# High and low weight halves interleaved word by word in one tile, so that the stationary operand is read with a step of two words

## The chip, the cores and the metric

The program runs on one NeuronCore of one Trainium2 chip, as one launch. The metric is the device time of that launch in microseconds; lower is better. The kernel before takes 2504.3 us, the median of 3 runs (2500.88 to 2507.38).

## What is computed

The reference chains two transformer stacks of two layers each over 512 tokens of width 1024 (528 with 16 meta tokens in the first stack). All arrays are float32. Cut to the products that matter here:

```
first:  h @ w_in_ab, attention with a top-k indexer, gated linear attention, @ w_out_ab
        h @ w_in_cd, retention, stick-breaking attention, @ w_out_cd
second: x = x + 0.5 * swiglu(rms_norm(x), w_gate, w_up, w_down)     # four times, width 2816
        x = x + pool_mla_mixer(...)      # layer 0
        x = x + gated_conv_mixer(...)    # layer 1
def swiglu(x, w_gate, w_up, w_down):
    return (jax.nn.silu(x @ w_gate) * (x @ w_up)) @ w_down
```

## The kernel before, in words

Activations live transposed: features on the 128 partitions, tokens along the free dimension (tiles `NH`, `NL`, `GH`, `GL`, `MH`, `ML`). The large products are all made with float32r operands, and each is split into three: with a weight w = wh + wl and an activation x = xh + xl, where the h part is the value rounded to float32r and the l part the rest, the kernel adds wh·xh + wh·xl + wl·xh in PSUM. A matmul and the weight load before it are written with one call; the first operand behind the output is the stationary one, which is loaded into the array (the PEld rows of the profile), the second is the moving one, which streams past it (the PE rows).

All weights are cut into blocks of up to 1024 rows by 256 columns (class `Block`, in the order of `weight_plan`). `raw`, `wh` and `wl` each have two slots; block b uses slot b % 2. For each block:

- SyncE's queue loads `raw` (`load_block`), once the low parts of block b - 2 are made.
- ScalarE (ACT) writes `wh` from `raw` with a Copy (`split_high`, L622: one instruction of up to 128x2048), once TensorE has finished block b - 2.
- GpSimd (POOL) writes `wl` = `raw` - `wh` (`split_low`, L641: four instructions of 128x512, two k tiles each), and counts `weights_low`.
- TensorE waits for `weights_low` and runs the block (`gemm`, `gemm_k`).

The form of a block says which operand is stationary and how wide the moving one is. In forms "F" (L667, 512 tokens), "W" (L660, 264 tokens, twice), "H" (L664, 264 tokens) and in `gemm_halves` (L689) the weights are stationary and the activations move. In forms "T0" and "T1" (L670) the activations are stationary and 256 columns of `wh` or `wl` move. Form "S" is a gate block of the swiglu products: it is made by the seven products of Strassen's scheme (`seven_pe`, L554), 84 matmuls with 256 moving tokens instead of 96. For it POOL and VectorE (DVE) first form sums of quarters of the weights in `ssum` (L509, L510, L515, L517), then ACT and POOL split the seven left operands (`seven_high`, L530; `seven_low`, L535): four of them into quarters of `wh` and `wl`, the other three into the tiles `swh` and `swl` (three quarters each). There are 36 such blocks, nine for each of the four swiglu stages, and each is followed by an "F" block of the up projection.

A block's steps sit in one queue per engine and in the order of the blocks, so ACT's and POOL's splits of block b + 1 run while TensorE works on block b. TensorE's instructions are in one fixed order, written out by the program. In every 512 token product the k loop is outermost and the three parts follow one another:

```
        for n, (w, x) in enumerate(((wh, hi), (wh, lo), (wl, hi))):
            ...
                last = nc.tensor.matmul(ps[0:m1 - m0, bank, 0:SEQ], w[:, s, k, m0:m1], x(k), start=start, stop=stop)
```

In `wh` and `wl` the 128 words of a stationary operand lie side by side in each partition.

Of the kernel before, what the change touches and what calls it, by code (L numbers as in the profile page):

```python
# [12 lines left out]
P = 128  # L13
# [248 lines left out]
def program(nc, inp, const_in, buckets_in, out, bias_line):  # L262
# [17 lines left out]

    H = at("H", 0, [P, KT, T])
    raw = at("raw", 4224, [P, 2, KT, BC])
    wh = at("wh", 8320, [P, 2, KT, BC], F32R)
    wl = at("wl", 12416, [P, 2, KT, BC], F32R)
    XA, XB = 16512, 20736
    K = [at("K0", 24960, [P, CONST_DATA[0].shape[1]]), None, None, None]
    gain = at("gain", 25600, [P, NROWS + 8])
# [137 lines left out]
    thi = at("thi", 34432, [P, 4, QT, QN], F32R)  # L425
    tsum = at("tsum", 30336, [P, 4, QT, QN])
    tlo = at("tlo", 30336, [P, 4, QT, QN], F32R)
    swh = at("swh", 38528, [P, 3, QT, P], F32R)
    swl = at("swl", 40064, [P, 3, QT, P], F32R)
    ssum = at("ssum", 41600, [P, 4, QT, P])  # L430
    xs = at("xs", 43648, [P, 3, QN])
    gcb = at("gcb", 29744, [P, 2, SEQ])
# [50 lines left out]
    def blk_cols(b):  # L483
        blk = BLOCKS[b]
        c0, n, to = blk.cols[-1]
        return to + n

    def seven_raw(b, name):
        row, col = int(name[1]) - 1, int(name[2]) - 1
        return raw[:, b % 2, QT * col:QT * col + QT, P * row:P * row + P]  # L490

    def seven_full(b, name):
        return seven_raw(b, name) if name[0] == "A" else ssum[:, int(name[1]) - 1, :, :]

    def seven_left(b, name, tile, extra):
        if name[0] == "A":
            row, col = int(name[1]) - 1, int(name[2]) - 1
            return tile[:, b % 2, QT * col:QT * col + QT, P * row:P * row + P]
        return tile[:, b % 2, 0:QT, P:2 * P] if name == "S1" else extra[:, int(name[1]) - 2, :, :]

    def seven_right(name, plain, formed):
        if name[0] == "B":
# [16 lines left out]
    def seven_high(act, b):  # L519
        n = SEVENS.index(b)  # L520
        act.wait_ge(S(f"raw_ready_{b % 2}"), RAWC[b])
        act.wait_ge(S("unit_done"), units_before(b - 1))
        for name in LEFT:
            if name == "S1":
                act.wait_ge(S("gate_sum"), 2 * n + 2)
            elif name == "S2":
                act.wait_ge(S("gate_mix"), 2 * n + 1)
            elif name == "S4":
                act.wait_ge(S("gate_mix"), 2 * n + 2)
            nc.scalar.activation(seven_left(b, name, wh, swh), seven_full(b, name), ACT.Copy).then_inc(S("weights_high"), 1)  # L530

    def seven_low(pool, b):
        for j, name in enumerate(LEFT):
            pool.wait_ge(S("weights_high"), HIGH_BEFORE[b] + j + 1)
            nc.gpsimd.tensor_tensor(seven_left(b, name, wl, swl), seven_full(b, name), seven_left(b, name, wh, swh).bitcast(F32),  # L535
                                    ALU.subtract).then_inc(S("weights_low"), 1)

    def seven_pe(pe, b, f, first):

        u, n = BLOCKS[b].unit0, SEVENS.index(b)  # L540
        for j, (left, right) in enumerate(zip(LEFT, RIGHT)):
            pe.wait_ge(S("weights_low"), LOW_BEFORE[b] + j + 1)
            if left == "A11":
                wait_slot(pe, u)
            elif left in ("S2", "S4", "S3"):
                pe.wait_ge(S("gate_copy"), 3 * n + ("S2", "S4", "S3").index(left) + 1)
            elif left == "A22":
                pe.wait_ge(S("gate_mid"), n + 1)
            if first and right[0] == "T":
                pe.wait_ge(S("formed_low"), 4 * f + T_ORDER.index(right) + 1)  # L550
            o = ps[:, ACCUMULATOR[j], 0:QN]
            for k in range(QT):
                for x, (w, e, plain, formed) in enumerate(((wh, swh, NH2, thi), (wh, swh, NL2, tlo), (wl, swl, NH2, thi))):
                    last = nc.tensor.matmul(o, seven_left(b, left, w, e)[:, k, :], seven_right(right, plain, formed)[:, k, :],  # L554
                                            start=left in ("A11", "S1", "A12") and k == 0 and x == 0,
                                            stop=k == QT - 1 and x == 2, skip_group_check=True)
# [54 lines left out]
    def split_high(act, b):  # L611

        if b >= len(BLOCKS):
            return
        if BLOCKS[b].form == "S":
            seven_high(act, b)
            return
        act.wait_ge(S(f"raw_ready_{b % 2}"), RAWC[b])
        if b >= 2:
            act.wait_ge(S("unit_done"), units_before(b - 1))  # L620
        k, w = BLOCKS[b].kts, blk_cols(b)
        nc.scalar.activation(wh[:, b % 2, 0:k, 0:w], raw[:, b % 2, 0:k, 0:w], ACT.Copy).then_inc(S("weights_high"), 1)  # L622

    def split_first_high(act, h):
        ks = slice(4 * h, 4 * h + 4)
        act.wait_ge(S("raw_ready_0" if h else "raw_first"), 16)
        nc.scalar.activation(wh[:, 0, ks, :], raw[:, 0, ks, :], ACT.Copy).then_inc(S("weights_high" if h else "first_high"), 1)

    def split_low(pool, b):
        if BLOCKS[b].form == "S":  # L630
            seven_sums_pool(pool, b)
            seven_low(pool, b)
            return
        if b:
            pool.wait_ge(S("weights_high"), HIGH_BEFORE[b + 1])
        k, w = BLOCKS[b].kts, blk_cols(b)
        for k0 in range(0, k, 2):
            if b == 0 and k0 % 4 == 0:
                pool.wait_ge(S("weights_high" if k0 else "first_high"), 1)
# [9 lines left out]
    def gemm_k(pe, b, i, k, hi, lo):  # L649

        blk = BLOCKS[b]
        s, total = b % 2, blk_cols(b)
        bank = bank_of(blk.unit0 + i)
        for n, (w, x) in enumerate(((wh, hi), (wh, lo), (wl, hi))):
            start, stop = k == 0 and n == 0, k == blk.kts - 1 and n == 2
            if blk.form == "W":
                m0, m1 = i * P, min(total, i * P + P)
                for h in range(2):
                    last = nc.tensor.matmul(ps[0:m1 - m0, bank + h, 0:T // 2], w[:, s, k, m0:m1],  # L660
                                            x(k)[:, h * (T // 2):(h + 1) * (T // 2)], start=start, stop=stop)
            elif blk.form == "H":
                m0, c0 = i // 2 * P, i % 2 * (T // 2)
                last = nc.tensor.matmul(ps[:, bank, 0:T // 2], w[:, s, k, m0:m0 + P], x(k)[:, c0:c0 + T // 2], start=start, stop=stop)  # L664
            elif blk.form == "F":
                m0, m1 = i * P, min(total, i * P + P)
                last = nc.tensor.matmul(ps[0:m1 - m0, bank, 0:SEQ], w[:, s, k, m0:m1], x(k), start=start, stop=stop)  # L667
            else:
                c0, n_tok = token_tile(i) if blk.form == "T1" else (i * P, P)
                last = nc.tensor.matmul(ps[0:n_tok, bank, 0:total], x(k)[:, c0:c0 + n_tok], w[:, s, k, 0:total], start=start, stop=stop)  # L670
        if k == blk.kts - 1:
            last.then_inc(S("unit_done"), 1)

    def gemm_halves(pe, b, hi, lo, ready):

        blk = BLOCKS[b]
        pe.wait_ge(S("weights_low"), LOW_BEFORE[b + 1])
        for i in range(2):
            wait_slot(pe, blk.unit0 + i)
        wide = blk.form == "W"  # L680
        w = T // 2 if wide else SEQ // 2
        for h in range(2):
            ready(pe, h)
            for i in range(2):
                bank = bank_of(blk.unit0 + i)
                o = ps[:, bank + h, 0:w] if wide else ps[:, bank, h * w:(h + 1) * w]
                for k in range(blk.kts):
                    for n, (weights, x) in enumerate(((wh, hi), (wh, lo), (wl, hi))):
                        last = nc.tensor.matmul(o, weights[:, b % 2, k, i * P:(i + 1) * P], x(k)[:, h * w:(h + 1) * w],  # L689
                                                start=k == 0 and n == 0, stop=k == blk.kts - 1 and n == 2)  # L690
                if h:
                    last.then_inc(S("unit_done"), 1)
# [2187 lines left out]
```

## Time and profile before

| | |
|---|---|
| runs | 2507.38, 2504.3, 2500.88 us |
| profiled execution | span 2503.9 us from its first to its last instruction; no other time is given for it |
| TensorE matmul (PE) | busy 2457.6 us, 98%, 14279 instructions |
| TensorE weight load (PEld) | busy 2087.2 us, 83%, 14279 instructions |
| GpSimd (POOL) | busy 1374.0 us, 55% |
| VectorE (DVE) | busy 1211.0 us, 48% |
| ScalarE (ACT) | busy 1007.4 us, 40% |
| mean granted TensorE clock | 0.995 of full speed |

Busy time of PE is from modelled ends: two matmuls in sequence overlap in the records, so a matmul's own duration says little, and the distance from one start to the next is what it costs the engine. The chain of waits, printed in order of time, merges the uninterrupted matmuls of one line into one row with their count; its microseconds divided by the count give that distance.

### The profile page before, as it was taken

The numbers are of one execution on the slowest core, as the hardware profiler recorded it, in microseconds if no ns is written. First come the engines' busy times: TensorE is split into PE (matmuls) and PEld (weight loads), VectorE is DVE, ScalarE is ACT, GpSimd is POOL, SyncE is SP. The second block draws the span as 40 slices with busy tenths as digits, with TensorE's granted clock in tenths as the row PEclk, the third lists the DMA queues.
The fourth block names the chain that finished last, engine by engine and source line by source line (L and its number), as shares of the span: only waits on it lengthen the run. The fifth ranks groups of instructions, "written<-read, shape, count | busy, mean of one in ns | idle before, by whom it ended". The sixth has DMA issues, their size and how long they took to land.

```text
span 2503.9 us, 35008 instructions
## 1 busy us (share of the span) xinstructions
PE 2457.6 (98%) x14279; PEld 2087.2 (83%) x14279; DVE 1211.0 (48%) x1948; ACT 1007.4 (40%) x1658; POOL 1374.0 (55%) x1010
## 2 busy tenths in 40 slices
PE   8999999999999999999999999999999999999999
PEld 7899779876678888877688988888988888888887
DVE  5666444245576242456573434462524543633333
ACT  4423444246563333437553433442423312433331
POOL 4233344421258686643167767586766454568673
PEclk9999999999999999999999999999999999999999
DMA  4223103210133333322123232323332322232322
GB/s 139 67 68 94 35 24 121 81 55 18 44 103 102 101 102 101 95 63 74 35 90 115 93 107 85 117 84 106 96 102 89 114 95 91 84 118 85 118 84 85
DMA packets 215881, 217.90 MB, mean 87 GB/s; under 512 B 10615, under 2 KB 213106, under 8 KB 215722
## 3 DMA queue, kind: packets, MB, share of 16 engines
q1 hardware_dynamic: 215520, 215.61, 27.1%
q8 instruction: 114, 1.87, 0.3%
q14 instruction: 45, 0.37, 0.0%
q10 hardware_dynamic: 202, 0.06, 0.0%
HBM read 213.53 MB, written 2.12 MB: 86 GB/s over the span
## 4 chain that ended last, share of the span: by engine, by line
PE 89%; DVE 5%; ACT 3%; POOL 1%; issue 1%; DMA 1%; SPq 0%; DVEq 0%; ACTq 0%
PE ps L667 53%; PE ps L554 14%; PE ps L660 6%; PE ps L670 5%; PE ps L664 2%; PE ps L1020 2%; ACT wh L622 1%; PE ps L1055 1%; POOL wl L641 1%; DVE tsum L599 1%; PE ps L1037 1%; PE ps L2317 1%; PE ps L2378 1%; PE ps L1818 1%; ACT bf L588 0%
## 5 line engine op out<-in xcount | busy, mean ns | idle before, releaser
L641 POOL TENSOR_TENSOR wl<-raw,wh 128x512 fp32r<-128x512 f32 (+1 forms) x650 | 863.9, 1359 | 1046.4 <-ACT wh L622 1031.7
L667 PE MATMUL ps<-NH,wh 128*128 128x512 f32 (+1 forms) x1248 | 493.3, 395 | 5.0 <-POOL wl L641 2.8
L667 PE MATMUL ps<-NL,wh 128*128 128x512 f32 (+1 forms) x1248 | 488.5, 391 | 0.0
L667 PE MATMUL ps<-NH,wl 128*128 128x512 f32 (+1 forms) x1248 | 487.6, 391 | 0.0
L622 ACT ACTIVATE wh<-raw 128x2048 fp32r<-128x2048 f32 (+5 forms) x182 | 310.6, 1707 | 430.5 <-PE ps L667 330.8
L667 PE MATMUL ps<-GH,wh 128*128 128x512 f32 x824 | 323.0, 392 | 0.0
L667 PE MATMUL ps<-GH,wl 128*128 128x512 f32 x824 | 320.7, 389 | 0.0
L667 PE MATMUL ps<-GL,wh 128*128 128x512 f32 x824 | 320.7, 389 | 0.0
L667 PEld LDWEIGHTS ps<-NH,wh 128*128 128x128 f32 (+1 forms) x1248 | 234.8, 188 | 61.0 <-issue 8.0
L667 PEld LDWEIGHTS ps<-NH,wl 128*128 128x128 f32 (+1 forms) x1248 | 234.7, 188 | 50.9
L667 PEld LDWEIGHTS ps<-NL,wh 128*128 128x128 f32 (+1 forms) x1248 | 234.8, 188 | 49.2 <-issue 1.4
L1292 DVE SCALAR_TENSOR_TENSOR H<-ps,H 128x512 f32<-128x512 f32 x96 | 66.4, 691 | 310.9 <-PE ps L667 310.8
L535 POOL TENSOR_TENSOR wl<-raw,wh 128x512 fp32r<-128x512 f32 x108 | 173.6, 1621 | 27.6 <-ACT wh L530 27.6
L667 PEld LDWEIGHTS ps<-GH,wh 128*128 128x128 f32 x824 | 154.7, 188 | 32.8 <-issue 1.0
L667 PEld LDWEIGHTS ps<-GH,wl 128*128 128x128 f32 x824 | 154.7, 188 | 32.3
L667 PEld LDWEIGHTS ps<-GL,wh 128*128 128x128 f32 x824 | 154.7, 188 | 31.4
L535 POOL TENSOR_TENSOR swl<-ssum,swh 128x512 fp32r<-128x512 f32 x108 | 154.2, 1459 | 0.0
L530 ACT ACTIVATE wh<-raw 128x512 fp32r<-128x512 f32 x108 | 63.7, 621 | 178.2 <-PE ps L667 72.0
L1284 DVE TENSOR_TENSOR GL<-tmp,GH 128x512 fp32r<-128x512 f32 x88 | 74.4, 845 | 102.2 <-ACT GH L1242 102.2
L1242 ACT ACTIVATE GH<-tmp 128x512 fp32r<-128x512 f32 x88 | 55.4, 629 | 158.8 <-DVE tmp L1282 158.7
L1282 DVE TENSOR_TENSOR tmp<-sg,tmp 128x512 f32<-128x512 f32 x88 | 88.7, 1008 | 36.3 <-ACT sg L1235 33.8
L670 PE MATMUL ps<-wh,NH 128*128 128x256 f32 (+1 forms) x320 | 90.9, 284 | 0.2 <-ACT dv L1995 0.2
(470 smaller groups left out, 5038.9 us busy)
## 6 DMA issues: line engine op xcount, KB each, us to landing
raw<-in_ffn_w_gate SPq DMA_DIRECT2D x44, 1024.0 KB, 5.3
raw<-in_ffn_w_up SPq DMA_DIRECT2D x44, 1024.0 KB, 5.3
raw<-in_ffn_w_down SPq DMA_DIRECT2D x32, 1024.0 KB, 5.1
raw<-in_w_in_ab SPq DMA_DIRECT2D x15, 1024.0 KB, 5.4
raw<-in_w_in_cd SPq DMA_DIRECT2D x14, 1024.0 KB, 5.0
raw<-in_ffn_w_down SPq DMA_DIRECT2D x16, 768.0 KB, 4.4
raw<-in_c_w_in SPq DMA_DIRECT2D x12, 1024.0 KB, 5.1
raw<-in_w_out_ab SPq DMA_DIRECT2D x8, 512.0 KB, 3.4
```

The source lines that it names most:

```text
L530: nc.scalar.activation(seven_left(b, name, wh, swh), seven_full(b, name), ACT.Copy).then_inc(S("weights_high"), 1)
L535: nc.gpsimd.tensor_tensor(seven_left(b, name, wl, swl), seven_full(b, name), seven_left(b, name, wh, swh).bitcast(F32), ALU.subtract).then ...
L554: last = nc.tensor.matmul(o, seven_left(b, left, w, e)[:, k, :], seven_right(right, plain, formed)[:, k, :], start=left in ("A11", "S1", " ...
L622: nc.scalar.activation(wh[:, b % 2, 0:k, 0:w], raw[:, b % 2, 0:k, 0:w], ACT.Copy).then_inc(S("weights_high"), 1)
L641: nc.gpsimd.tensor_tensor(wl[:, b % 2, ks, 0:w], raw[:, b % 2, ks, 0:w], wh[:, b % 2, ks, 0:w].bitcast(F32), ALU.subtract).then_inc(S("wei ...
L660: last = nc.tensor.matmul(ps[0:m1 - m0, bank + h, 0:T // 2], w[:, s, k, m0:m1], x(k)[:, h * (T // 2):(h + 1) * (T // 2)], start=start, sto ...
L667: last = nc.tensor.matmul(ps[0:m1 - m0, bank, 0:SEQ], w[:, s, k, m0:m1], x(k), start=start, stop=stop)
L670: last = nc.tensor.matmul(ps[0:n_tok, bank, 0:total], x(k)[:, c0:c0 + n_tok], w[:, s, k, 0:total], start=start, stop=stop)
L1242: nc.scalar.activation(GH[:, 2 * p_ + i, :], tmp[:, i, 0:SEQ], ACT.Copy).then_inc(S("hidden_high"), 1)
L1282: nc.vector.tensor_tensor(tmp[:, i, 0:SEQ], sg[:, i, :], tmp[:, i, 0:SEQ], ALU.mult).then_inc(S("hidden"), 1)
L1284: nc.vector.tensor_tensor(GL[:, 2 * p_ + i, :], tmp[:, i, 0:SEQ], GH[:, 2 * p_ + i, :].bitcast(F32), ALU.subtract).then_inc(S("hidden_low" ...
L1292: nc.vector.scalar_tensor_tensor(out=H[:, m, META:T], in0=ps[:, bank_of(u), :], scalar=0.5, in1=H[:, m, META:T], op0=ALU.mult, op1=ALU.add ...
```

## The change

The two tiles `wh` and `wl` become one piece of memory of the same size at the same place. For each slot it is seen in two ways: `w_pairs`, in which word 2c is the high half and word 2c + 1 the low half of column c, and `w_rows`, in which all high words of a slot lie in front of all its low words. `weights_of(b, low)` takes `w_rows` for the forms T0 and T1, where the weights are the moving operand, and `w_pairs` for every other form. `swh` and `swl` become `sw_pairs` in the same way. So in the forms F, W, H and S each stationary operand is 128 words at a step of two words; ACT's Copy writes at that step; POOL's subtraction reads the high halves and writes the low ones at that step, and reads `raw` or `ssum` as before. The number of instructions on each engine, their order, their element counts and their waits stay as they were.

```diff
-    wh = at("wh", 8320, [P, 2, KT, BC], F32R)
-    wl = at("wl", 12416, [P, 2, KT, BC], F32R)
+    w_pairs = at("w_pairs", 8320, [P, 2, KT, BC, 2], F32R)
+    w_rows = at("w_rows", 8320, [P, 2, 2, KT, BC], F32R)
...
-    swh = at("swh", 38528, [P, 3, QT, P], F32R)
-    swl = at("swl", 40064, [P, 3, QT, P], F32R)
+    sw_pairs = at("sw_pairs", 38528, [P, 3, QT, P, 2], F32R)
...
+    def weights_of(b, low):
+        return w_rows[:, b % 2, low, :, :] if BLOCKS[b].form[0] == "T" else w_pairs[:, b % 2, :, :, low]
+
...
-    def seven_left(b, name, tile, extra):
+    def seven_left(b, name, low):
+        tile = weights_of(b, low)
         if name[0] == "A":
             row, col = int(name[1]) - 1, int(name[2]) - 1
-            return tile[:, b % 2, QT * col:QT * col + QT, P * row:P * row + P]
-        return tile[:, b % 2, 0:QT, P:2 * P] if name == "S1" else extra[:, int(name[1]) - 2, :, :]
+            return tile[:, QT * col:QT * col + QT, P * row:P * row + P]
+        return tile[:, 0:QT, P:2 * P] if name == "S1" else sw_pairs[:, int(name[1]) - 2, :, :, low]
...
-        nc.scalar.activation(wh[:, b % 2, 0:k, 0:w], raw[:, b % 2, 0:k, 0:w], ACT.Copy).then_inc(S("weights_high"), 1)
+        nc.scalar.activation(weights_of(b, 0)[:, 0:k, 0:w], raw[:, b % 2, 0:k, 0:w], ACT.Copy).then_inc(S("weights_high"), 1)
...
-            nc.gpsimd.tensor_tensor(wl[:, b % 2, ks, 0:w], raw[:, b % 2, ks, 0:w], wh[:, b % 2, ks, 0:w].bitcast(F32), ALU.subtract).then_inc(S("weights_low"), 1)
+            nc.gpsimd.tensor_tensor(weights_of(b, 1)[:, ks, 0:w], raw[:, b % 2, ks, 0:w], weights_of(b, 0)[:, ks, 0:w].bitcast(F32), ALU.subtract).then_inc(S("weights_low"), 1)
...
-        for n, (w, x) in enumerate(((wh, hi), (wh, lo), (wl, hi))):
+        for n, (low, x) in enumerate(((0, hi), (0, lo), (1, hi))):
+            w = weights_of(b, low)
...
-                last = nc.tensor.matmul(ps[0:m1 - m0, bank, 0:SEQ], w[:, s, k, m0:m1], x(k), start=start, stop=stop)
+                last = nc.tensor.matmul(ps[0:m1 - m0, bank, 0:SEQ], w[:, k, m0:m1], x(k), start=start, stop=stop)
```

## Rows read from the trace of the kernel before

**Rows 1.** The page: span, busy time per engine, granted TensorE clock
```profile
span 2503.9 us, 35008 instructions
...
PE 2457.6 (98%) x14279; PEld 2087.2 (83%) x14279; DVE 1211.0 (48%) x1948; ACT 1007.4 (40%) x1658; POOL 1374.0 (55%) x1010
...
PEclk9999999999999999999999999999999999999999
```

**Rows 2.** The page: the chain that ended last, by engine and line
```profile
PE 89%; DVE 5%; ACT 3%; POOL 1%; issue 1%; DMA 1%; SPq 0%; DVEq 0%; ACTq 0%
PE ps L667 53%; PE ps L554 14%; PE ps L660 6%; PE ps L670 5%; PE ps L664 2%; PE ps L1020 2%; ACT wh L622 1%; PE ps L1055 1%; POOL wl L641 1%; DVE tsum L599 1%; PE ps L1037 1%; PE ps L2317 1%; PE ps L2378 1%; PE ps L1818 1%; ACT bf L588 0%
```

**Rows 3.** TensorE's waits: engine, line, waited for, us, times, longest
```profile
PE ps L667 <- POOL wl L641: 2.8, 6, 1.0
```

**Rows 4.** Chain in order of time: start us, us, what
```profile
458.70 19.48 PE ps L667 x84
478.19 23.48 PE ps L660 x192
...
1303.92 10.07 PE ps L554 x84
1313.99 10.91 PE ps L667 x48
...
1334.97 54.43 PE ps L667 x240
...
1170.05 1.75 PE ps L1657 x16
```

**Rows 5.** Groups, PE by shape (line, names, sizes, count | busy us, mean ns)
```profile
L667 PE MATMUL ps<-NH,wh 128*128 128x512 f32 x1240 | 490.1, 395 | 5.0 <-POOL wl L641 2.8 <-DVE NL L777 2.2
...
L667 PE MATMUL ps<-GH,wh 128*128 128x512 f32 x824 | 323.0, 392 | 0.0
...
L554 PE MATMUL ps<-thi,swh 128*128 128x256 f32 x288 | 81.6, 283 | 3.5 <-ACT xs L566 2.0 <-issue 1.5
...
L660 PE MATMUL ps<-NH,wh 128*128 128x264 f32 x304 | 64.9, 295 | 2.7 <-DVE agT L1979 2.7
...
L554 PE MATMUL ps<-NH,swh 128*128 128x256 f32 x144 | 40.8, 283 | 0.0
...
L664 PE MATMUL ps<-NH,wh 128*128 128x264 f32 x128 | 38.9, 304 | 0.0
...
L660 PE MATMUL ps<-MH,wh 128*128 128x264 f32 x112 | 25.8, 312 | 0.1
```

**Rows 6.** Groups, weight loads (PEld) by shape
```profile
L667 PEld LDWEIGHTS ps<-GL,wh 128*128 128x128 f32 x824 | 154.7, 188 | 31.4
...
L670 PEld LDWEIGHTS ps<-wh,NH 128*16 128x16 f32 x64 | 6.0, 94 | 2.1 <-issue 0.8
```

**Rows 7.** Timeline of POOL over one S and F pair, 1510 to 1531 us
```profile
1510.10 3.79 POOL L535 TENSOR_TENSOR swl<-ssum,swh 128x512 fp32r<-128x512 f32 x3
1513.86 2.53 POOL L535 TENSOR_TENSOR wl<-raw,wh 128x512 fp32r<-128x512 f32 x2
1518.93 5.05 POOL L641 TENSOR_TENSOR wl<-raw,wh 128x512 fp32r<-128x512 f32 x4 [2.54 <-ACT wh L622]
1523.94 1.29 POOL L509 TENSOR_TENSOR ssum<-raw 128x512 f32<-128x512 f32 x1
1525.19 1.29 POOL L510 TENSOR_TENSOR ssum<-raw 128x512 f32<-128x512 f32 x1
1527.72 1.74 POOL L535 TENSOR_TENSOR wl<-raw,wh 128x512 fp32r<-128x512 f32 x1 [1.24 <-ACT wh L530]
1529.42 1.74 POOL L535 TENSOR_TENSOR wl<-ssum,wh 128x512 fp32r<-128x512 f32 x1
```

**Rows 8.** Timeline of ACT, the same pair
```profile
1516.94 1.91 ACT L622 ACTIVATE wh<-raw 128x2048 fp32r<-128x2048 f32 x1 [5.72 <-PE ps L667]
...
1527.01 0.63 ACT L530 ACTIVATE wh<-raw 128x512 fp32r<-128x512 f32 x1 [5.44 <-PE ps L554]
```

More of the change, by code:

```diff
@@ L529, in seven_high @@
                 act.wait_ge(S("gate_mix"), 2 * n + 2)
-            nc.scalar.activation(seven_left(b, name, wh, swh), seven_full(b, name), ACT.Copy).then_inc(S("weights_high"), 1)
+            nc.scalar.activation(seven_left(b, name, 0), seven_full(b, name), ACT.Copy).then_inc(S("weights_high"), 1)
     def seven_low(pool, b):
@@ L534, in seven_low @@
             pool.wait_ge(S("weights_high"), HIGH_BEFORE[b] + j + 1)
-            nc.gpsimd.tensor_tensor(seven_left(b, name, wl, swl), seven_full(b, name), seven_left(b, name, wh, swh).bitcast(F32),
+            nc.gpsimd.tensor_tensor(seven_left(b, name, 1), seven_full(b, name), seven_left(b, name, 0).bitcast(F32),
                                     ALU.subtract).then_inc(S("weights_low"), 1)
@@ L552, in seven_pe @@
             for k in range(QT):
-                for x, (w, e, plain, formed) in enumerate(((wh, swh, NH2, thi), (wh, swh, NL2, tlo), (wl, swl, NH2, thi))):
-                    last = nc.tensor.matmul(o, seven_left(b, left, w, e)[:, k, :], seven_right(right, plain, formed)[:, k, :],
+                for x, (low, plain, formed) in enumerate(((0, NH2, thi), (0, NL2, tlo), (1, NH2, thi))):
+                    last = nc.tensor.matmul(o, seven_left(b, left, low)[:, k, :], seven_right(right, plain, formed)[:, k, :],
                                             start=left in ("A11", "S1", "A12") and k == 0 and x == 0,
@@ L626, in split_first_high @@
         act.wait_ge(S("raw_ready_0" if h else "raw_first"), 16)
-        nc.scalar.activation(wh[:, 0, ks, :], raw[:, 0, ks, :], ACT.Copy).then_inc(S("weights_high" if h else "first_high"), 1)
+        nc.scalar.activation(weights_of(0, 0)[:, ks, :], raw[:, 0, ks, :], ACT.Copy).then_inc(S("weights_high" if h else "first_high"), 1)
     def split_low(pool, b):
@@ L652, in gemm_k @@
         blk = BLOCKS[b]
-        s, total = b % 2, blk_cols(b)
+        total = blk_cols(b)
         bank = bank_of(blk.unit0 + i)
-        for n, (w, x) in enumerate(((wh, hi), (wh, lo), (wl, hi))):
+        for n, (low, x) in enumerate(((0, hi), (0, lo), (1, hi))):
+            w = weights_of(b, low)
             start, stop = k == 0 and n == 0, k == blk.kts - 1 and n == 2
@@ L659, in gemm_k @@
                 for h in range(2):
-                    last = nc.tensor.matmul(ps[0:m1 - m0, bank + h, 0:T // 2], w[:, s, k, m0:m1],
+                    last = nc.tensor.matmul(ps[0:m1 - m0, bank + h, 0:T // 2], w[:, k, m0:m1],
                                             x(k)[:, h * (T // 2):(h + 1) * (T // 2)], start=start, stop=stop)
@@ L663, in gemm_k @@
                 m0, c0 = i // 2 * P, i % 2 * (T // 2)
-                last = nc.tensor.matmul(ps[:, bank, 0:T // 2], w[:, s, k, m0:m0 + P], x(k)[:, c0:c0 + T // 2], start=start, stop=stop)
+                last = nc.tensor.matmul(ps[:, bank, 0:T // 2], w[:, k, m0:m0 + P], x(k)[:, c0:c0 + T // 2], start=start, stop=stop)
             elif blk.form == "F":
                 m0, m1 = i * P, min(total, i * P + P)
-                last = nc.tensor.matmul(ps[0:m1 - m0, bank, 0:SEQ], w[:, s, k, m0:m1], x(k), start=start, stop=stop)
+                last = nc.tensor.matmul(ps[0:m1 - m0, bank, 0:SEQ], w[:, k, m0:m1], x(k), start=start, stop=stop)
             else:
                 c0, n_tok = token_tile(i) if blk.form == "T1" else (i * P, P)
-                last = nc.tensor.matmul(ps[0:n_tok, bank, 0:total], x(k)[:, c0:c0 + n_tok], w[:, s, k, 0:total], start=start, stop=stop)
+                last = nc.tensor.matmul(ps[0:n_tok, bank, 0:total], x(k)[:, c0:c0 + n_tok], w[:, k, 0:total], start=start, stop=stop)
         if k == blk.kts - 1:
@@ L687, in gemm_halves @@
                 for k in range(blk.kts):
-                    for n, (weights, x) in enumerate(((wh, hi), (wh, lo), (wl, hi))):
-                        last = nc.tensor.matmul(o, weights[:, b % 2, k, i * P:(i + 1) * P], x(k)[:, h * w:(h + 1) * w],
+                    for n, (low, x) in enumerate(((0, hi), (0, lo), (1, hi))):
+                        last = nc.tensor.matmul(o, weights_of(b, low)[:, k, i * P:(i + 1) * P], x(k)[:, h * w:(h + 1) * w],
                                                 start=k == 0 and n == 0, stop=k == blk.kts - 1 and n == 2)
```

## The prediction

> **What bounds the kernel now.** I read the page first, then the chain of waits, then the distance from matmul to matmul. On the page TensorE is busy 98% of the span and its clock is granted in full in every slice [rows 1], so neither another engine nor the clock holds the kernel back. The chain that ended last lies on PE for 89%, and three quarters of the span are the four lines whose stationary operand the change touches: L667, L554, L660 and L664 [rows 2]. TensorE hardly waits for the engine that finishes the weights: 2.8 us in all at L667 [rows 3]. So the time moves only if one matmul becomes dearer or cheaper, or if the splits get so slow that TensorE starts to wait for them.
>
> What does one matmul cost? Dividing the pieces of the chain by their counts: 54.43 / 240 = 226.8 ns for 512 moving columns, 10.07 / 84 = 119.9 ns for 256, 23.48 / 192 = 122.3 ns for 264 [rows 4]. At the granted 2.4 GHz one column per cycle gives 213.3, 106.7 and 110.0 ns. So each of these matmuls costs 12.3 to 13.5 ns more than its columns, whatever its width. Two rows say what kind of cost this is. 
>
> **The mechanism I forecast.** A weight load of 128 columns lasts 188 ns, one of 16 columns 94 ns [rows 6]: (188 - 94) / 112 = 0.84 ns per column, half the pace of the moving stream (0.42 ns per column). Both read four bytes per column from the same partitions. At a step of one word the moving read thus runs through addresses twice as fast as the stationary read and passes it again and again; if the two collide where they meet in the same part of the memory, that is a loss that depends on addresses, as seen. At a step of two words the stationary read covers eight bytes per 0.84 ns, exactly the moving read's speed: they keep their distance and collide once per load at most. The slow transposes, where the streams have another ratio of speeds, show about what is left.
>
> The Trainium skill speaks against this (TensorE: Matmul & The Clock Gate, Step-by-step: what each phase is for): TensorE has two independent read ports, and loading the next weights takes no read bandwidth from the running matmul. By that rule the gain is 0 and the time 2504 us; it is the first rival. The 5 ns that hang on the address alone do not agree with it.
>
> **The change part by part.**
> - Stationary reads at two words. Matmuls concerned: L667 3 x (1240 + 824) = 6192, L554 9 x 288 + 3 x 144 = 3024, L660 3 x (304 + 112) = 1248, L664 3 x 128 = 384 [rows 5]; 10848 in all. Each group's partners with the other two parts have the same count; some 360 in small groups are left out. The price is not in the trace, so from both sides: gain at most 13.4 - 2.7 = 10.7 ns each (116 us), at least 0; a loss is not excluded either, and is priced under the rivals. I take 9 ns, near the upper end, because the nearest row is the transposes' and I leave 1.7 ns for the one collision at a load's start: 10848 x 9 ns = 98 us. All of it lies on the path, since these lines are the chain.
> - L670 (weights moving) stays at a step of one word on both sides: nothing.
> - ACT's writes at two words. The F split takes 1.91 us for 2048 columns, the seven S splits 0.63 us each [rows 8]. Lower bound: no change. Upper bound, doubled: the F split ends 1.9 us later, the first S split 0.6 us later. Both push POOL, which idles 2.54 us before the one and 1.24 us before the other [rows 7]. I take nothing; the cover is POOL's idle time.
> - POOL's reads and writes at two words. In one pair of an S and an F block (10.07 + 10.91 = 21.0 us of TensorE [rows 4]) POOL spends 3.79 + 2.53 + 5.05 + 1.74 + 1.74 = 14.9 us on splits and 2.6 us on sums, and idles 3.8 us [rows 7]. After the forecast gain the pair is 132 x 9 ns = 1.2 us shorter and the idle time 2.6 us: still enough. The same POOL instruction on 128x512 takes 1.27 us in some rows and 1.74 us in others [rows 7], so its bounds are 0 and, if all pay the dear price, (1.74 - 1.27) x 11 = 5.2 us at most, of which part is paid already. I take nothing. What would be late next is the first low part of the S block.
> - DVE, the DMA queues, the waits and the order are as before: nothing.
>
> Sum: 2503.9 - 98 = 2406 us. The median of the runs, 2504.3, is 0.4 us above the span, which changes nothing. Own range of this case: 2385 us (10.7 ns, with the small groups) to 2465 us (a third of the loss goes).
>
> **Rivals.**
> 1. *No change, 2504 us.* The 13 ns are a fixed price of a float32r matmul whose weights are exchanged. For it: L554 with 256 columns and L667 with 512 lose the same, although the streams meet for different times; against it: 231.9 beside 226.8 ns. A measurement here can tell some 0.3% (8 us) from nothing. ACT and POOL as above stay hidden. The Trainium skill (SBUF — State Buffer, A bandwidth-pool intuition that's wrong, the box on cachelines) says that fp32 may be strided for free while two accesses fall in one 16-byte line, which a step of two words just keeps; no row here has such a step.
> 2. *More collisions, about 2600 us.* A step of two words touches twice the stretch of memory per load. If each stretch costs the moving read something, the loss grows: by 5.1 ns as between 226.8 and 231.9 (+55 us, 2559) or by another 13.4 ns (+145 us, 2649). Against it: a load of few columns does not make its neighbours free.
> 3. *The splits become the bound, about 2630 us.* Place: POOL in the S and F pairs. It decides from 3.8 / 14.9 = 26% on. At 50% dearer the splits add 7.4 us, 3.6 us of it uncovered, in 36 pairs: +130 us. TensorE would stand before L554 or L667 waiting for the low parts. Against it: one word per element is moved either way.
> 4. *The weight load becomes the bound, about 3000 us.* If a column at two words takes 1.68 instead of 0.84 ns, 128 take 215 ns and with the 13 ns no matmul can follow in less than 228. The 512-column ones stay (226.8), but 4656 of 256 or 264 columns pay 107 ns more: +498 us. It decides once 128 columns take over 120 ns, 12% more than now.
>
> **How the numbers follow.** Forecast case 50%, no change 24%, more collisions 9%, POOL 10%, weight load 7%. The likeliest case gives 2406 us. The range runs from 2375, a little below the full removal, over the forecast case and the unchanged time to 2560, the mild end of rival 2; above it lie the dear ends, rivals 3 and 4, some 20%. Faster by over 0.3%: 0.50; within: 0.24; slower: 0.26.
>
> **What would show it.** In the chain in order of time, 240 matmuls of L667's successor should take about 52.3 us instead of 54.43, 84 of L554's about 9.3 instead of 10.07, and the stretch of the first stack's F blocks (231.9 ns) should fall most. L670's distance stays. POOL's and ACT's mean durations should stay within 25% and TensorE's waits for the low parts within a few us. Wrong if the distances stay at 226.8 and 119.9 (rival 1), rise (rivals 2 and 4; in rival 4 the 256-column ones alone, with loads far over 188 ns), or if waits for POOL appear (rival 3).

## The result, and the profile after

The change makes the kernel slower: 2552.72 us, the median of 4 runs (2550.02 to 2556.5), against 2505.16 us of the kernel before beside it (2500.88 to 2507.38). The ratio is 1.0196, with a 95% interval of 1.0182 to 1.021. I had forecast 2406 us. The time moved the other way. The range holds it only at its far end, beside the mild end of rival 2 (2559 us).

The page of the kernel after, in the same parts as [rows 1]:

```profile
span 2551.6 us, 35008 instructions
...
PE 2505.3 (98%) x14279; PEld 2138.9 (84%) x14279; DVE 1210.4 (47%) x1948; ACT 1041.2 (41%) x1658; POOL 1393.7 (55%) x1010
...
PEclk9999999999999999999999999999999999999999
```

TensorE has 47.7 us more of busy time, and the span is 47.7 us longer (2551.6 - 2503.9). The clock is granted as before. Its chain and its wait for the low parts, to compare with [rows 2, 3]; L671, L557, L664 and L674 are the old L667, L554, L660 and L670:

```profile
PE 92%; DVE 4%; ACT 2%; issue 1%; POOL 1%; DMA 1%; SPq 0%; DVEq 0%; ACTq 0%
...
PE ps L671 <- POOL w_pairs L644: 1.8, 3, 0.8
```

PE's share of the chain grew from 89 to 92%, and the wait for POOL's low parts shrank from 2.8 to 1.8 us. So nobody is waited for more; TensorE's own work is dearer. Which matmuls are dearer is read from the chain in order of time (start, us, what), as [rows 4]:

```profile
458.83 19.51 PE ps L671 x84
478.34 23.58 PE ps L664 x192
...
1319.70 10.08 PE ps L557 x84
1329.77 11.31 PE ps L671 x48
...
1351.16 56.53 PE ps L671 x240
...
2006.13 179.19 PE ps L671 x768
```

- 512 columns in the swiglu stages: 56.53 / 240 = 235.5 ns, before 226.8: +8.8 ns.
- 512 columns elsewhere in the second stack: 179.19 / 768 = 233.3 ns. The same piece of the kernel before reads:

```profile
1972.57 174.11 PE ps L667 x768
```

  174.11 / 768 = 226.7 ns, so here it is +6.6 ns.
- 512 columns in the first stack, where the moving tile starts at word 16: 19.51 / 84 = 232.3 ns, before 231.9.
- 256 columns: 120.0 ns, before 119.9. 264 columns: 122.8 ns, before 122.3.

This adds up. Each of four swiglu stages has 960 such matmuls from its first S block on (nine up blocks of 48; eight down blocks of 48 and four of 36): 3840 x 8.8 = 34 us. Some 1950 others of 512 columns in the second stack: x 6.6 = 13 us. That is 47 of the 47.7 us. The starts of the same matmuls in the two traces, compared one by one, give 45.6 us for the 512 columns, 1.2 for 264 and 0.2 for 256.

The engines that write the halves, by groups. The first two rows are the kernel after, where the blocks of the forms T0 and T1 stand in a group of their own (`w_rows`), so its counts are lower:

```profile
L644 POOL TENSOR_TENSOR w_pairs<-raw,w_pairs 128x512 fp32r<-128x512 f32 x600 | 817.1, 1394 | 933.6 <-ACT w_pairs L625 920.2 <-ACT w_pairs L630 13.4
...
L625 ACT ACTIVATE w_pairs<-raw 128x2048 fp32r<-128x2048 f32 x125 | 260.8, 2086 | 335.2 <-PE ps L671 284.7 <-DMA raw<-in_ffn_w_down 25.4 <-PE ps L664 18.8
```

```profile
L641 POOL TENSOR_TENSOR wl<-raw,wh 128x512 fp32r<-128x512 f32 x639 | 854.4, 1367 | 1034.5 <-ACT wh L622 1019.8 <-ACT wh L627 13.4 <-DVE mx L1103 1.2
...
L622 ACT ACTIVATE wh<-raw 128x2048 fp32r<-128x2048 f32 x133 | 253.9, 1909 | 358.5 <-PE ps L667 277.7 <-PE ps L660 39.2 <-DMA raw<-in_ffn_w_down 29.3
```

ACT pays 9% for writing at two words (2086 against 1909 ns), POOL 2% (1394 against 1367 ns). A weight load went from 188 [rows 6] to 196 ns:

```profile
L671 PEld LDWEIGHTS ps<-GL,w_pairs 128*128 128x128 f32 x824 | 161.3, 196 | 30.3
```

### The profile page after: what moved, and what is told of

Its sections match the earlier page's. It is cut to its first block, busy times and chain, and to the rows that moved or that the text cites. A ratio compares the mean times of both kernels' runs of the same rounds, so it can differ in the third digit from the quotient of the medians.

```text
span 2551.6 us, 35008 instructions
## 1 busy us (share of the span) xinstructions
PE 2505.3 (98%) x14279; PEld 2138.9 (84%) x14279; DVE 1210.4 (47%) x1948; ACT 1041.2 (41%) x1658; POOL 1393.7 (55%) x1010
## 4 chain that ended last, share of the span: by engine, by line
PE 92%; DVE 4%; ACT 2%; issue 1%; POOL 1%; DMA 1%; SPq 0%; DVEq 0%; ACTq 0%
PE ps L671 57%; PE ps L557 14%; PE ps L664 6%; PE ps L674 4%; PE ps L668 2%; PE ps L1024 2%; PE ps L1059 1%; PE ps L1041 1%; PE ps L2321 1%; PE ps L2382 1%; PE ps L1822 1%; ACT w_pairs L625 0%; PE ps L693 0%; DVE tlo L612 0%; PE ps L2167 0%
## 5 line engine op out<-in xcount | busy, mean ns | idle before, releaser
L644 POOL TENSOR_TENSOR w_pairs<-raw,w_pairs 128x512 fp32r<-128x512 f32 (+1 forms) x608 | 824.1, 1388 | 945.1 <-ACT w_pairs L625 931.6
L671 PE MATMUL ps<-NH,w_pairs 128*128 128x512 f32 (+1 forms) x2496 | 805.2, 399 | 3.6 <-POOL w_pairs L644 1.8
L671 PEld LDWEIGHTS ps<-NH,w_pairs 128*128 128x128 f32 (+1 forms) x2496 | 487.0, 195 | 109.9 <-issue 7.8
L671 PE MATMUL ps<-GH,w_pairs 128*128 128x512 f32 x1648 | 529.8, 400 | 0.0
L671 PE MATMUL ps<-NL,w_pairs 128*128 128x512 f32 (+1 forms) x1248 | 493.9, 396 | 0.0
L625 ACT ACTIVATE w_pairs<-raw 128x2048 fp32r<-128x2048 f32 (+2 forms) x167 | 316.8, 1898 | 389.2 <-PE ps L671 321.4
L671 PEld LDWEIGHTS ps<-GH,w_pairs 128*128 128x128 f32 x1648 | 323.8, 196 | 66.2 <-issue 1.0
L671 PE MATMUL ps<-GL,w_pairs 128*128 128x512 f32 x824 | 326.2, 396 | 0.0
L671 PEld LDWEIGHTS ps<-NL,w_pairs 128*128 128x128 f32 (+1 forms) x1248 | 243.1, 195 | 47.5 <-issue 1.4
L538 POOL TENSOR_TENSOR w_pairs<-raw,w_pairs 128x512 fp32r<-128x512 f32 x108 | 177.3, 1655 | 27.4 <-ACT w_pairs L533 27.4
L671 PEld LDWEIGHTS ps<-GL,w_pairs 128*128 128x128 f32 x824 | 161.3, 196 | 30.3
L557 PE MATMUL ps<-thi,sw_pairs 128*128 128x256 f32 x576 | 115.5, 283 | 3.5 <-ACT xs L569 2.0
L674 PE MATMUL ps<-w_rows,NH 128*128 128x256 f32 (+1 forms) x640 | 117.1, 282 | 0.2 <-ACT dv L1999 0.2
L557 PE MATMUL ps<-thi,w_pairs 128*128 128x256 f32 x576 | 115.5, 283 | 0.0
L557 PE MATMUL ps<-NH,w_pairs 128*128 128x256 f32 x576 | 115.4, 283 | 0.0
L664 PE MATMUL ps<-NH,w_pairs 128*128 128x264 f32 (+1 forms) x640 | 112.5, 292 | 2.7 <-DVE agT L1983 2.7
```

Source lines behind the costliest of these rows:

```text
L538: nc.gpsimd.tensor_tensor(seven_left(b, name, 1), seven_full(b, name), seven_left(b, name, 0).bitcast(F32), ALU.subtract).then_inc(S("weig ...
L557: last = nc.tensor.matmul(o, seven_left(b, left, low)[:, k, :], seven_right(right, plain, formed)[:, k, :], start=left in ("A11", "S1", "A ...
L625: nc.scalar.activation(weights_of(b, 0)[:, 0:k, 0:w], raw[:, b % 2, 0:k, 0:w], ACT.Copy).then_inc(S("weights_high"), 1)
L644: nc.gpsimd.tensor_tensor(weights_of(b, 1)[:, ks, 0:w], raw[:, b % 2, ks, 0:w], weights_of(b, 0)[:, ks, 0:w].bitcast(F32), ALU.subtract).t ...
L671: last = nc.tensor.matmul(ps[0:m1 - m0, bank, 0:SEQ], w[:, k, m0:m1], x(k), start=start, stop=stop)
```

## The experiments

The theory after the result (A): a stationary read at two words still disturbs the moving read, more than one at one word does when both tiles start where they do here; the loss lies in TensorE's two reads alone. The rivals: (B) ACT's and POOL's writes at two words disturb TensorE's reads; (C) the weight load lasts so long that it sets the pace; (D) the new places of the halves in memory do it.

### e1_streams: the two reads with no other engine

A kernel that leaves out the reference's computation and holds series of 48 matmuls alone, in the operand pattern of the kernel (hi, lo, hi against high, high, low). ACT and POOL stand still while a series runs; only the step, the width or a start varies.

```
for step, low, n, cols, start in configs:
    for i, k, (base, x_) in ...:            # 2 x 8 x 3
        a = step * (k * 256 + i * 128) % 4096 + base
        matmul(ps[0:cols, c % 2, 0:n], w[:, a:a + cols * step:step], x_[:, k * 512 + start:k * 512 + start + n])
```

> Leaves out the whole computation; it only runs 48-matmul series, with a pause between them, on float32r operands that lie where the kernel's do (stationary words at w, moving ones at hi and lo, all at the same start modulo 2048 bytes), with the same order hi, lo, hi. Series in order: one at step 1 to warm up; then widths 512, 384, 264, 256, 128, each at stationary steps 1, 2, 4; then width 512 with the moving tiles shifted by 4, 8, 16, 32, 48, 64 words, each at steps 1 and 2; then 64 and 32 stationary columns at steps 1 and 2; then step 2 with the low half 4096, 8, 0 words away, step 1 with the low half at 0 and 4096 words, and step 2 with it at 1 word. Theory A (the two reads of TensorE meet more often at a step of two): without any other engine at work step 2 gives 233 to 236 ns per matmul at width 512 against 226.8 at step 1, and 120 for both at width 256; step 4 more than step 2. Theory B (the interleaved writes of ACT and POOL disturb TensorE): step 1 and step 2 are equal here, 226.8 ns. Fixed price theory: all shifts of the moving tile give the same distance; theory A expects it to change with the shift, by about 5 ns as between 226.8 and 231.9.

The chain in order of time of this kernel; L84 is a step of one word, L86 of two, L88 of four. The three rows of a width stand together, for 512, 256 and 128 columns:

```profile
37.92 11.19 PE ps L84 x48
...
49.41 11.48 PE ps L86 x48
...
61.18 11.69 PE ps L88 x48
...
127.55 6.02 PE ps L84 x48
...
133.88 6.05 PE ps L86 x48
...
140.22 11.49 PE ps L88 x48
...
152.01 5.59 PE ps L84 x48
...
157.90 5.88 PE ps L86 x48
...
164.08 11.48 PE ps L88 x48
```

A piece also holds a longer first step and the tail of its last matmul (0.54 us together at 512 columns), so distances are taken between starts, without the first ones. At 512 columns they are 226.7 ns at one word and 233.3 at two: the +6.6 ns of the kernel after, without ACT, POOL or a DMA at work. At 256 columns 120 and 120, at 384 columns 173.3 and 173.3, at 264 columns 121.3 and 123.2, at 128 columns 111.7 and 117.9. With the moving tile shifted by 4 to 48 words the step of one word itself costs 228.8 to 233.4 ns; shifted by 64 words it is back at 226.7. And with 64 stationary columns the step of two is the cheaper one, 226.7 against 229.8 ns. The distance between high and low half (4096, 8, 1 or 0 words) changes nothing. At four words every width costs 233 to 235 ns, as if something other than the moving columns set the pace. The load is longer there:

```profile
L88 PEld LDWEIGHTS ps<-hi,w 128*128 128x128 f32 x160 | 45.1, 325 | 2.9 <-ACT junk L68 2.9
```

It lasts 325 ns instead of 194 at two words and 193 at one. So a pace set by the load fits the series at four words, and not those at two, where 256 columns still cost 120 ns. That it is the load at four words is inferred from its length.

### e2_reads: before, with the read at two words alone

The halves stay apart and contiguous; F, W, H and `gemm_halves` load 128 words at a step of two from them, so these products use the columns of a block in another order than the reference.

```diff
+    def stepped(w, s, k, m0, m1, total):
+        return w[:, s, k, m0 // P:2 * P:2] if total == 2 * P else w[:, s, k, m0:m1]
```

> The kernel before with its layout and its writes; only in forms F, W and H the stationary operand is read at a step of two words inside the old rows: the first tile of 128 takes the even columns, the second the odd ones, so columns of the products come out permuted. Theory A: all or nearly all of the loss is there, 2545 to 2555 us, 233 to 236 ns per matmul at L667. Theory B and the placement theory: 2504 us and 226.8 ns.

Measured: 2539.12 us, ratio 1.0143 (1.0128 to 1.0158). The F blocks cost 233.2 ns without any interleaved write (L670 is the old L667):

```profile
1343.36 55.98 PE ps L670 x240
```

### e3_writes: after, with the read at one word

ACT and POOL write at two words as in the kernel after, but F, W, H and `gemm_halves` load 128 neighbouring words, which are high and low halves mixed, so these products are taken with the mixed columns. S blocks stay at two words.

```diff
+    def plain(w, b, k, low, m0, m1, total):
...
+        at_ = m0 + 2 * P * low
+        return w_pairs[:, b % 2, k, :, :].rearrange("p c t -> p (c t)")[:, at_:at_ + P]
```

> The changed kernel with its interleaved writes; only in forms F, W and H TensorE reads 128 neighbouring words of the interleaved rows, high and low mixed, so the products are of mixed halves. Theory A: about 2504 us and 226.8 ns per matmul with 512 columns. Theory B: 2545 to 2555 us. Placement theory: the same.

Measured: 2508.91 us, ratio 1.0018 (1.0007 to 1.003). ACT is as dear as in the kernel after, and TensorE is at its old distance (54.43 / 240 = 226.8):

```profile
L625 ACT ACTIVATE w_pairs<-raw 128x2048 fp32r<-128x2048 f32 x125 | 259.9, 2079 | 319.7 <-PE ps L677 271.0 <-DMA raw<-in_ffn_w_down 28.2 <-PE ps L670 18.7
```

```profile
1336.81 54.43 PE ps L677 x240
```

This refutes B but for 0.2% (4 to 5 us). Writes beside reads that are both at two words are compared further down (e6_s_rows).

### e4_place: after, with all halves in rows

```diff
-        return w_rows[:, b % 2, low, :, :] if BLOCKS[b].form[0] == "T" else w_pairs[:, b % 2, :, :, low]
+        return w_rows[:, b % 2, low, :, :]
```

> The changed kernel with the row view for every form: nothing is interleaved, but the halves lie where the change puts them (both halves of one slot side by side). Theories A and B: 2504 us. Placement theory (it is the new start addresses): 2545 to 2555 us.

Measured: 2503.89 us, ratio 1.0002 (0.9988 to 1.0016). The new places alone cost nothing; D is refuted.

### e5_grid: starts, mixtures, two-byte operands

Like e1_streams, without the reference's computation and with series of 24: 64 combinations of the starts of stationary, hi and lo (0, 16, 32, 48 words) at either step; a narrow series (84 of 256 columns, L98) and a wide one (96 of 512, L104) without a pause; bf16 operands (L112); a moving operand at one and two words (L119).

> Leaves out the whole computation; series of matmuls alone. Two series to warm up, then 64 series of 24 float32r matmuls of 512 columns at a stationary step of 1 and 64 at a step of 2, each with another start of the stationary words, of the high and of the low moving words (0, 16, 32 or 48 words past a multiple of 64, high moving tile outside, low inside, stationary outermost); then other stationary starts (4, 8, 12, 24, 40, 56 words); then steps 3, 1, 2; then four mixed series without a pause, 84 matmuls of 256 columns followed by 96 of 512, with the steps 1 1, 1 2, 2 1, 2 2; then bfloat16 operands at stationary steps 1 and 2 and widths 512 and 256; then float32r with the moving operand at steps 1 and 2, 256 columns. Theory A (collisions that depend on the distance of the two reads): over the 64 starts the distance varies from about 226.7 to 234 ns at step 1 and no start brings step 2 under 226.7; in the mixed series the wide part costs 235.5 ns after a narrow part at step 2 and 233.3 after one at step 1. Theory F (a fixed price per float32r matmul, to which a step of two adds a fixed one): the starts change nothing. The lockstep theory of the forecast: some starts at step 2 give 216 to 220 ns. For bfloat16, theory A has no firm number: 216 ns if the loss belongs to four-byte words, 227 if to every weight load.

At one word the 64 combinations give 226.7 ns (the three starts equal, and only then) to 234.5; at two words 228.8 to 233.3, in no case less. Mostly the starts relative to each other count: of 32 groups of four series with the same differences of starts, some 26 agree within 1 ns, and in the others the four differ by up to 3.5 ns. The stationary start alone is enough: 16 words later, with both moving tiles at 0, a step of one costs 233.4 ns instead of 226.7, and a step of two 230.0 instead of 233.3. The high moving tile 48 words later does the same. The first two rows are a step of one, with all starts at 0 and with the high moving one at 48 (226.7 and 234.6 ns); the other two are the same starts at a step of two (233.3 and 228.9 ns):

```profile
41.24 5.75 PE ps L89 x24
...
114.71 5.89 PE ps L89 x24
...
433.50 5.88 PE ps L89 x24
...
507.31 5.80 PE ps L89 x24
```

The mean over the 64 combinations is 231.0 ns at one word and 231.3 at two, by the starts of the matmuls in this trace. Leaving out differences of up to 0.3 ns, two words are cheaper at some 27 of the 64 and dearer at some 26. So over these starts the step itself costs next to nothing in the mean; the kernel before, with all its starts equal in the second stack, stood at one of the four combinations that favour a step of one most.

The narrow and wide series, in the order of steps (1, 1), (1, 2), (2, 1), (2, 2):

```profile
919.26 10.34 PE ps L98 x84
929.60 21.80 PE ps L104 x96
...
962.03 22.40 PE ps L104 x96
...
995.08 21.80 PE ps L104 x96
...
1027.53 22.62 PE ps L104 x96
```

The wide matmuls cost 226.7, 233.3, 226.7 and 235.6 ns. So 233.3 or 235.6 depends on what ran before: a narrow series at two words makes the wide one at two words dearer by 2.3 ns for its whole length of 96 matmuls. These are the two prices of the kernel after. In bf16 a matmul costs 216 ns with 512 columns and 109 with 256 at either step (24 take 2.81 us with 256 columns at two words), about 2.5 ns over its bare columns instead of 13. So at the one set of starts that was run in bf16, the larger loss belongs to operands of four bytes; other starts were not run in bf16.

```profile
1056.12 2.81 PE ps L112 x24
...
1064.90 2.81 PE ps L112 x24
...
1068.01 3.15 PE ps L119 x24
...
1071.46 5.71 PE ps L119 x24
```

The last two rows are 256 float32r columns moving at one and at two words: 120 and 226.6 ns. Had the change not kept `w_rows` for T0 and T1, whose weights move, those matmuls could be expected to pay this; no run tried it in the kernel.

### e6_s_rows and e7_s_only: S blocks apart from the rest

e6_s_rows is the kernel after with S blocks in rows; e7_s_only is the kernel after with S blocks alone interleaved and all else in rows.

```diff
-        return w_rows[...] if BLOCKS[b].form[0] == "T" else w_pairs[...]
+        return w_rows[...] if BLOCKS[b].form[0] in "TS" else w_pairs[...]   # e6_s_rows
+        return w_rows[...] if BLOCKS[b].form != "S" else w_pairs[...]       # e7_s_only
```

> The changed kernel, but with the gate blocks of form S in the row view (not interleaved); forms F, W and H stay interleaved. If the 235.5 ns per matmul in the swiglu stages come from S blocks read at a step of two just before (another state in which the wide series starts), L671 takes 233.3 ns everywhere and the time is 2540 to 2545 us. If they come from the interleaved writes beside the interleaved reads of the F blocks themselves, it stays at 235.5 ns and 2550 to 2553 us.

> The changed kernel, but only the gate blocks of form S are interleaved; all other forms use the row view. Theory A: matmuls with 256 columns cost 120 ns at either step, so 2503 to 2510 us, the latter if the entry state makes the wide matmuls that follow dearer. Rival 4 of the forecast (the weight load becomes the bound) expects them far over 120 ns and 2800 us or more.

e6_s_rows: 2543.95 us, ratio 1.0156 (1.0142 to 1.017). The F blocks fall to 55.98 / 240 = 233.2 ns:

```profile
1351.81 55.98 PE ps L671 x240
```

e7_s_only: 2503.32 us, ratio 1.0002 (0.9993 to 1.0011). 256-column matmuls stay at 120 ns, and the F blocks behind them, at one word, at 226.8:

```profile
1322.40 10.10 PE ps L557 x84
1332.50 54.43 PE ps L671 x240
```

So the S blocks cost nothing themselves, and rival 4 of the prediction is refuted; but at two words they make the F blocks at two words that follow them dearer. The trace of the kernel after shows the same in two more places: before its first S block its F blocks stand 233.3 ns apart, and at the end of a swiglu stage, after 216 matmuls at 50.87 / 216 = 235.5 ns, two matmuls of L816 are enough to bring the 768 that follow at 2006 us back to 233.3:

```profile
1954.26 50.87 PE ps L671 x216
2005.13 1.00 PE ps L816 x2
```

### e8_pairs_moved and e9_rows_moved: the same two moves in either kernel

`NH2` starts 48 words later and `GH` 16 words earlier, in the kernel after (e8) and in the kernel before (e9).

```diff
-    NH2 = at("NH2", XA, [P, KT, SEQ], F32R)
+    NH2 = at("NH2", XA + 48, [P, KT, SEQ], F32R)
...
-    GH = at("GH", GA + 40, [P, KT, SEQ], F32R)
+    GH = at("GH", GA + 24, [P, KT, SEQ], F32R)
```

> The changed kernel; only the high moving tiles of the second stack start elsewhere, NH2 48 words later and GH 16 words earlier, so both lie 48 words past a multiple of 64 while the low moving tiles and the weights stay at one. In the series at a step of two this start had the least loss, 228.8 ns. If the loss hangs on the starts of the two reads, L671 falls from 235.5 and 233.3 to about 229 ns in the second stack: some 5700 matmuls x 4.5 to 6.5 ns, 2518 to 2527 us. If the step costs a fixed amount, it stays at 2552 us.

> The kernel before, nothing interleaved, with the same two tiles moved in the same way. In the series at a step of one this start cost 234.4 ns against 226.7. If the loss hangs on the starts, L667 rises to about 234 ns in the second stack and the time to 2540 to 2550 us without any step of two; if a step of one is free of it, 2504 us.

e8: 2523.3 us, ratio 1.0077 (1.0062 to 1.0092), less than half of the change's loss. e9: 2538.77 us, ratio 1.0139 (1.0122 to 1.0156), with no step of two words anywhere. The F blocks of each:

```profile
1344.45 54.95 PE ps L671 x240
```

```profile
1342.33 56.26 PE ps L667 x240
```

229.0 ns at two words, 234.4 at one: at these starts the order of the two steps is turned round, as in the same four rows of e5_grid. What the change lost is in the main no price of the step as such, but of how the two reads meet at these starts.

### e10_starts, e11_all_moved, e12_formed_moved: a better start?

e10_starts: again only series, of 24 at one word, 256 combinations of the starts of hi and lo in steps of 4 words, with 512 and with 256 columns.

> Leaves out the whole computation; 512 series of 24 float32r matmuls at a stationary step of one, 256 with 512 columns and then 256 with 256 columns, the stationary words at a multiple of 64 and the high (outer loop) and low (inner loop) moving words 0, 4, 8 ... 60 words past one. It looks for a start that beats both kernels. If all starts of both reads together on a multiple of 64 words are the best there is, no series of 512 columns lies under 226.7 ns; a start near 220 ns would be worth some 40 us in the kernel. At 256 columns the kernel has 120.0; the trial with moved tiles had 118.7, so some starts should be at or under that.

512 columns: 226.6 to 236.6 ns, mean 231.8. 256 columns: 113.4 to 120.2, mean 118. With both starts at 0, where the kernel before has all its tiles of the second stack (multiples of 64 words), 512 columns cost 226.8 ns, within 0.2 ns of the least there is, and 256 columns 119.4 to 120, near the most. With both at word 28, 512 columns cost 226.7 and 256 columns 113.4:

```profile
772.53 5.72 PE ps L83 x24
```

```profile
2020.82 3.02 PE ps L83 x24
```

e11_all_moved takes this to the kernel before: right operands of the second stack 28 words later, the formed left ones 64 words later. e12_formed_moved moves only the formed operands of the S blocks.

```diff
-    thi = at("thi", 34432, [P, 4, QT, QN], F32R)
+    thi = at("thi", 34460, [P, 4, QT, QN], F32R)
...
-    tlo = at("tlo", 30336, [P, 4, QT, QN], F32R)
+    tlo = at("tlo", 30364, [P, 4, QT, QN], F32R)
...
-    NH2 = at("NH2", XA, [P, KT, SEQ], F32R)      # e11_all_moved alone,
+    NH2 = at("NH2", XA + 28, [P, KT, SEQ], F32R) # and NL2, GH, GL likewise
```

> The kernel before, nothing interleaved; all moving tiles of the second stack (NH2, NL2, GH, GL, thi, tlo, and what is formed in their place) start 28 words later, while the weights stay at multiples of 64 words (swh, swl, ssum and xs 64 words later). In the series alone this start had 226.6 ns at 512 columns and 113.4 ns at 256 (against 226.7 and 120.0 with all on a multiple of 64). If that holds beside the other engines and across the change from 256 to 512 columns: 36 blocks of 84 matmuls x 6.6 ns = 20 us less, 2484 us. If the state in which a series starts matters more than the series itself, L554 takes between 113.4 and 120 and L667 between 226.7 and 234 ns, 2490 to 2530 us.

> The kernel before, nothing interleaved; only the formed operands of the S blocks (thi, tlo and what is formed in their place) start 28 words later, NH2, NL2, GH and GL stay at multiples of 64 words. The last trial had 113.3 ns at L554's 256 columns but 231.1 at L667's 512. If the start alone counts, 48 of the 84 matmuls of an S block take 113.3 ns and 36 take 120, and L667 stays at 226.7: 36 x 48 x 6.6 ns = 11 us less, 2492 us. If the state carried over from the S block counts, L667 leaves 226.7 and the gain is gone: 2500 to 2530 us.

e11: 2507.96 us, ratio 1.0012 (1.0002 to 1.0022). The S blocks gained as hoped (9.52 / 84 = 113.3 ns), but the F blocks lost it again (55.47 / 240 = 231.1 ns, where the series at this start had 226.7):

```profile
1332.61 55.47 PE ps L671 x240
1388.07 9.52 PE ps L558 x84
...
1969.96 177.49 PE ps L671 x768
```

The S blocks are not the reason. The 768 matmuls of the last row follow two matmuls of L816 and cost 177.49 / 768 = 231.1 ns as well, and the F blocks before the first S block of the kernel stand 231.2 ns apart. What makes 231.1 of 226.7 here stays open; the series had 24 matmuls, one tile of 128 weight columns per k tile and no other engine at work, and no run separates these.

e12: 2499.56 us against 2505.04 beside it, ratio 0.9983 (0.9974 to 0.9992): a little faster than both kernels, with 54.43 and 9.92 us in the same rows. The F blocks keep their 226.8 ns beside the moved S blocks. An S matmul costs 9.92 / 84 = 118.1 ns in the mean, where the expectation gives (48 x 113.3 + 36 x 120) / 84 = 116.2, so the gain is 4 to 5 us instead of 11.

```profile
1329.29 54.43 PE ps L671 x240
1383.72 9.92 PE ps L558 x84
```

## Why the prediction was wrong, step by step

**What bounds the kernel: right.** The time moved only through the price of a matmul; waits for POOL did not appear.

**"The loss depends on where in memory the two operands lie": right.** e9_rows_moved loses 1.4% by two start addresses alone, and e1_streams shows the loss with every other engine at rest. The Trainium skill says that TensorE has two independent read ports and that loading the next weights takes no read bandwidth from the running matmul (TensorE: Matmul & The Clock Gate, Step-by-step: what each phase is for). These runs do not agree for float32r: the same instruction costs 226.6 to 236.6 ns by addresses alone, and 226.7 or 233.4 by the stationary start alone (e5_grid).

**"Stationary reads at two words", 10848 x 9 ns = 98 us gained: the step that failed.** Instead of 9 ns gained, a matmul measured 0 ns at 256 columns, +0.5 at 264, +0.4 at 512 in the first stack, and +6.6 or +8.8 at 512 in the second: 47 us lost. Two parts of it were wrong:

- The equal speed of the two reads. I took 0.84 ns per stationary column from two load durations, and concluded that at eight bytes per column the reads keep their distance. If they did, some start should come near the bare columns (213.3 ns). In e5_grid none at two words is under 228.8. The ratio of speeds was inference; no row showed reads in step.
- The nearest row. The transposes of L1657 (2.7 ns lost) set the upper bound, and 9 ns was taken by their side. They differ from these matmuls in more than the ratio of speeds: they load 96 stationary columns, in 126 ns, where L667 loads 128 in 188 ns. The row at 458 us, for the same instruction, showed that an altered address pattern costs 5.1 ns more.

And one question was left out: how good the starts of before are among all starts. e5_grid and e10_starts answer it: with all tiles on multiples of 64 words, 512 columns at a step of one are within 0.2 ns of the least of 256 starts, and of the 64 starts at a step of two none is under 228.8. So the change could only lose there (L667, 53% of the chain [rows 2], but for its stretch in the first stack). Over the 64 starts of e5_grid the two steps cost nearly the same in the mean, 231.0 and 231.3 ns.

**Rival 2, "more collisions": nearest.** Its price, 5.1 ns on every matmul, was too low for 512 columns and too high for the narrow ones; the two errors cancel (2559 against 2552.7 us). Its reason, a longer stretch of memory, isn't shown: in e8_pairs_moved the same stretch costs 229.0 ns.

**Where the 2% come from**, by ratios: the reads at two words 1.0143 (e2_reads), the writes 1.0018 (e3_writes; between e2_reads and e6_s_rows it is 0.0013), the state left by S blocks 0.004 (1.0196 - 1.0156), the places 0 (e4_place). 0.0143 + 0.0013 to 0.0018 + 0.004 = 0.0196 to 0.0201, against 0.0196. The lower sum meets the total by construction, as each term is the difference of two runs; the check is that e3_writes gives nearly the same for the writes by another way.

**ACT's and POOL's writes, taken as nothing: nearly right.** ACT pays 9%, far from the doubling that bounded it, POOL 2%; by e3_writes 4 to 5 us reach the end (0.07 to 0.3%). **The forms T, nothing: right**, because of `w_rows`. **Rival 3** did not occur. **Rival 4**: a load at two words is 4% longer, not 12%, and the matmuls with 256 columns stayed at 120 ns.

**Open.** What in the memory makes the losses, several of which are near multiples of 6.7 ns (213.3 bare, then 226.7 and 233.3), while others are not (228.8, 231.1); why even the best start loses 13 ns at 512 columns; what TensorE carries from a narrow series at two words into a wide one; and why the F blocks of e11_all_moved cost 231.1 ns and not 226.7. The runs show each, and explain none.

## What to carry to other kernels

A float32r matmul whose weights are exchanged each time costs up to 4% more at 512 columns, and up to 6% more at 256, by the starts of its two operands (226.6 to 236.6 and 113.4 to 120.2 ns in e10_starts); divide the chain's pieces by their counts, and treat every change of layout as a change of these starts. Before changing a pattern, ask whether the present one is already at its best. Measure a series alone at the width in use, and then try its best start in the kernel, as the series can promise what the kernel does not give (e11_all_moved). A mechanism inferred from two durations should not outweigh a row of the same instruction that points the other way.

## What the runs showed that I had not expected

- The best starts differ with the width: both at word 28 give 113.4 ns for 256 columns against 120 at word 0, while 512 columns cost 226.7 or 226.8 ns at either.
- At two words a series' price depends on the series before it, for as long as 240 matmuls: 233.3 or 235.6 ns (e5_grid, e6_s_rows). At one word no such effect is seen: 226.7 ns behind a narrow series at either step (e5_grid).
- The step is nearly free for the load up to two words and dear behind it: 193 ns at one word and 194 at two in the series (188 and 196 in the kernels), 253 at three (e5_grid), 325 at four. The Trainium skill (SBUF — State Buffer, Door 1: The DMA port swizzle, the box on cachelines, which the prediction names under another section) says that two hits in one 16-byte line give full bandwidth, and that crossing to a new line costs. At two words, which keeps two hits, the load agrees; for the moving operand the trace disagrees, since it costs 226.6 ns instead of 120 at two words.
